# A four-layer transformer forward pass on one core: stage ends of the first layer type removed, work moved between stages and engines

## The chip, the cores and the metric

The kernel is one program for one core of a Trainium2 chip. Time is device time in microseconds (us), taken per execution. TensorE is called PE, VectorE DVE, ScalarE ACT, GpSimd POOL, and SP is the queue that loads weights from HBM. A PE row in the trace is one or more matmuls of one source line.

## The reference

A batch of one sequence with 512 tokens and model width 1024 passes through two layers of a first type and two of a second type. In the first type the input projection feeds three mixers, whose outputs are joined, projected and added to x, and an MLP follows:

```
def first_block(x, ...):
    for l in range(DEPTH):
        h = rms_norm(x, norm_mix[l])
        z = h @ w_in[l]
        (q_a, k_a, v_a, q_h, i_h, f_fw, f_bw, g_h, a_c, g_c) = jnp.split(z, splits, axis=-1)
        ...
        o_att = block_attention(q_a, k_a, v_a)              # 8 heads of 64, softmax over 512 keys
        o_hg = hgrn2_bidirectional(q_h, i_h, f_fw, f_bw, g_h, ...)   # 4 heads of 64, both directions
        o_cv = conformer_conv(a_c, g_c, conv_w[l], ...)     # 31 taps on 256 channels
        mix = jnp.concatenate([o_att, o_hg.astype(x.dtype), o_cv], axis=-1)
        x = x + mix @ w_out[l]
        h = rms_norm(x, norm_mlp[l])
        x = x + jnp.square(jax.nn.relu(h @ w_mlp_in[l])) @ w_mlp_out[l]
```

The recurrence, S_t = diag(f_t) S_{t-1} + k_t v_t and o_t = S_t^T q_t, runs forwards and backwards; the sum of both is normalised per head and multiplied by silu(g). The second type has four mixers (among them a gated linear recurrence with one direction and two attentions with masks), a gated sum of them, and an MLP. Everything is float32.

## The kernel before

**Tiles.** Activations lie transposed, features on the 128 partitions and the 512 tokens along the free dimension. A projection tile is 8 blocks of the contraction, three matmuls each: weights and activations are split into a high and a low part (`hH`, `hL`, `w_hi`, `w_lo`) and three of the four products are summed. ACT makes `w_hi` (L231), POOL `w_lo` (L261), one unit of 128 x 1024 at a time, three units ahead of PE. DVE takes each finished tile out of the two accumulators `acc` (`evacuate`), and PE may write an accumulator again when `acc_free` has counted that.

**Order.** Every engine has its own instruction stream, in the order in which the Python code issues it, and waits on semaphores. There is no scheduler: what stands behind a waiting instruction waits too.

**A layer of the first type** (`first_layer`) goes through these stages. `first_in`, 12 tiles: inputs of the convolution, forget gates, and q and v of the recurrence. DVE puts 30 of the 62 convolution taps behind these tiles (`CONV_EARLY`). Then two turns: PE transposes the recurrence's v tiles `Z[10]` and `Z[11]` into token order (`turn_pe`, L736) and ACT copies them back (`turn_act`, L744). Then the recurrence in two runs (`Recurrence`), run r on heads 2r and 2r+1. A run has 19 steps: for each direction nine levels with half width h = 256, 128, 64, ..., 1, and one last step for the diagonal. In a step with half width h, DVE subtracts a reference column from the summed log decays `cum` (the gap, L829), ACT takes its exponential (L880), DVE multiplies q and k by it (L838), PE makes the scores (L910), and two steps later DVE keeps them in `near` or `SS` (L857, L866). The levels with h = 256 and 128 are the far ones. Beside run 0 PE computes six tiles of `late_in` (the attention's q, k, v), which get their norm and rotation there (`rope_pe`, `norm_act`, `rope_dve`), beside run 1 the last two (the gate g). Each run ends with the products with the values (`pe_values`, L921).

**Turn to attention.** After run 1 every stream computes what is left of the heads' norms: PE sums squares (L1137, L1142), ACT makes the reciprocal roots (L1239, L1240), DVE multiplies and splits (L1360 to L1363, L435, L436). Then `finish` drains each engine and `after` makes each wait for the other two. Then PE turns the attention's v tile `Z[5]` and ACT copies it.

**Attention** (`PairAttention`) goes through 16 slots, four query blocks for each of four pairs of heads. In slot s, PE makes the scores of both heads (L585), DVE their negated maxima (L709), ACT the exponentials with their sums (L656). DVE in slot s+1 takes the reciprocal (L715) and scales both heads' rows (L720), PE in slot s+2 transposes them (L612), ACT copies (L675). After four slots PE makes the products with v (L629), and DVE takes the output of the pair (`take_output`, L1099, L1100). Beside slots 0 to 10 DVE puts the 32 remaining taps (L1288). The convolution's layer norm is spread over slots 11 to 15. No tile of a projection runs beside this attention. Then `out` and the MLP follow.

**The second type** uses the same classes: `Recurrence` with one direction beside `fox_in`, and `PairAttention` beside `stick_in` and `gate3`.

## Time and profile before

| | |
|---|---|
| time, median of 3 runs | 3814.58 us (3814.35 to 3814.77) |
| the profiled execution's own time | 3813.89 us |
| its span | 3812.6 us |
| mean granted PE clock | 0.977 of full speed |
| PE busy | 3653.6 us, 96% |
| DVE busy | 2175.0 us, 57% |
| ACT busy | 1305.1 us, 34% |
| chain that ended last | PE 83%, DVE 13%, issue 3%, ACT 2% |

Layer 0 of the first type fills about the first 750 us, and layer 1 repeats it about 700.6 us later. The clock is given as a share of 2.4 GHz, and 0.50 is 1.2 GHz. Rows of the timeline that follow each other overlap by some 0.08 us, so a DVE instruction of 0.69 us takes 0.60 of its stream.

### The profile page before, as it was taken

How to read it: one execution, taken by the hardware profiler on the slowest of the kernel's cores; microseconds unless marked ns; L12 is line 12 of the kernel's file. 1: busy time of each engine (PE TensorE's matmuls, PEld its weight loads, DVE VectorE, ACT ScalarE, POOL GpSimd, SP SyncE). 2: the span in 40 equal slices, each digit the busy share in tenths (PEclk: the TensorE clock that was granted, in tenths of full speed). 3: DMA queues.
4: the chain of work that ended last, by engine and by line, in shares of the span. 5: the costliest groups of instructions: out<-in, count | busy, mean ns of one | idle time of the engine just before them, and what ended most of it. 6: DMA issues, size and time to landing. Idle time of an engine off the chain costs nothing.

```text
span 3812.6 us, 44671 instructions
## 1 busy us (share of the span) xinstructions
PE 3653.6 (96%) x17862; PEld 2809.7 (74%) x17862; DVE 2175.0 (57%) x3018; ACT 1305.1 (34%) x2217; POOL 1292.0 (34%) x522
## 2 busy tenths in 40 slices
PE   8889999987899999999999999999999999999998
PEld 6646888865488888677777678887767777778887
DVE  7887565698764474633274485555553255365445
ACT  5345121343521122435333432123354433442212
POOL 3102444430044443132333244444213232334443
PEclk9889999997999999999999999999999999999999
DMA  4101333310033334122222133334112121223332
GB/s 137 40 12 45 97 97 96 94 61 23 13 96 97 96 98 136 34 63 60 78 62 76 52 88 100 94 100 145 57 34 78 58 81 61 67 72 94 99 94 83
DMA packets 81373, 292.38 MB, mean 77 GB/s; under 512 B 9712, under 2 KB 11152, under 8 KB 80656
## 3 DMA queue, kind: packets, MB, share of 16 engines
q1 hardware_dynamic: 78384, 278.49, 23.9%
q10 hardware_dynamic: 2784, 11.03, 0.9%
q8 instruction: 143, 2.34, 0.3%
q14 instruction: 62, 0.51, 0.0%
HBM read 285.30 MB, written 2.10 MB: 75 GB/s over the span
## 4 chain that ended last, share of the span: by engine, by line
PE 83%; DVE 13%; issue 3%; ACT 2%; DMA 0%; SPq 0%; DVEq 0%; ACTq 0%
PE acc L317 23%; PE acc L319 22%; PE acc L318 22%; PE banks L629 2%; PE banks L585 2%; PE banks L910 2%; DVE conv_c L1288 2%; PE banks L612 2%; PE banks L921 1%; DVE gap L829 1%; DVE QK L838 1%; DVE stat L709 1%; PE banks L1536 1%; DVE pair L387 1%; DVE probs L720 1%
## 5 line engine op out<-in xcount | busy, mean ns | idle before, releaser
L261 POOL TENSOR_TENSOR w_lo<-w_raw,w_hi 128x1024 fp32r<-128x1024 f32 x518 | 1291.8, 2495 | 2490.4 <-ACT w_hi L231 2490.4
L231 ACT ACTIVATE w_hi<-w_raw 128x1024 fp32r<-128x1024 f32 x518 | 548.7, 1060 | 1712.6 <-PE acc L319 1659.9
L317 PE MATMUL acc<-hH,w_hi 128*128 128x512 f32 x1776 | 731.9, 412 | 18.5 <-DVE sig L1921 6.6
L319 PE MATMUL acc<-hL,w_hi 128*128 128x512 f32 x1776 | 699.6, 394 | 0.0
L318 PE MATMUL acc<-hH,w_lo 128*128 128x512 f32 x1776 | 698.8, 393 | 0.0
L317 PEld LDWEIGHTS acc<-hH,w_hi 128*128 128x128 f32 x1776 | 337.5, 190 | 107.0 <-issue 32.9
L317 PE MATMUL acc<-H,w_hi 128*128 128x512 f32 x1024 | 400.4, 391 | 3.8 <-DVE L L379 3.8
L350 DVE TENSOR_TENSOR xT<-acc,xT 128x512 f32<-128x512 f32 x160 | 110.6, 691 | 514.3 <-PE acc L319 495.7
L317 PE MATMUL acc<-midH,w_hi 128*128 128x512 f32 x1024 | 400.3, 391 | 0.3
L318 PE MATMUL acc<-midH,w_lo 128*128 128x512 f32 x1024 | 398.7, 389 | 0.0
L319 PE MATMUL acc<-midL,w_hi 128*128 128x512 f32 x1024 | 398.5, 389 | 0.0
L319 PE MATMUL acc<-L,w_hi 128*128 128x512 f32 x1024 | 398.4, 389 | 0.0
L318 PE MATMUL acc<-H,w_lo 128*128 128x512 f32 x1024 | 398.4, 389 | 0.0
L319 PEld LDWEIGHTS acc<-hL,w_hi 128*128 128x128 f32 x1776 | 337.2, 190 | 73.8
L318 PEld LDWEIGHTS acc<-hH,w_lo 128*128 128x128 f32 x1776 | 338.3, 191 | 66.4 <-issue 4.3
L317 PEld LDWEIGHTS acc<-midH,w_hi 128*128 128x128 f32 x1024 | 192.2, 188 | 46.6 <-DVE midL L477 7.0
L317 PEld LDWEIGHTS acc<-H,w_hi 128*128 128x128 f32 x1024 | 192.2, 188 | 46.0 <-DVE L L379 5.5
L318 PEld LDWEIGHTS acc<-H,w_lo 128*128 128x128 f32 x1024 | 192.2, 188 | 40.6 <-issue 1.0
L319 PEld LDWEIGHTS acc<-midL,w_hi 128*128 128x128 f32 x1024 | 192.2, 188 | 40.2
L319 PEld LDWEIGHTS acc<-L,w_hi 128*128 128x128 f32 x1024 | 192.2, 188 | 40.0
L318 PEld LDWEIGHTS acc<-midH,w_lo 128*128 128x128 f32 x1024 | 192.3, 188 | 39.4
L476 DVE CAST midH<-relu_sb 128x512 fp32r<-128x512 f32 x64 | 160.2, 2504 | 2.2
(324 smaller groups left out, 4722.7 us busy)
## 6 DMA issues: line engine op xcount, KB each, us to landing
w_raw<-in_stream SPq DMA_DIRECT2D x518, 512.0 KB, 3.6
cw<-in_cmpw ACTq DMA_DIRECT2D x2, 2048.0 KB, 7.2
mixed<-in_cmpw ACTq DMA_DIRECT2D x2, 2048.0 KB, 12.7
x_tok<-in_x SPq DMA_DIRECT2D x2, 1024.0 KB, 7.3
out<-f_tok SPq DMA_DIRECT2D x8, 256.0 KB, 2.1
stack<-Z ACTq DMA_DIRECT2D x8, 128.0 KB, 2.3
stack<-Z ACTq DMA_DIRECT2D x8, 127.8 KB, 2.5
masks_f<-in_masks SPq DMA_DIRECT2D x1, 960.0 KB, 11.7
```

Of the source, the lines that this page charges most:

```text
L231: act.activation(w_hi[:, u % WB, 0:w], w_raw[:, u % 2, 0:w], ACT.Copy).then_inc(hi_split, 1)
L261: pool.tensor_tensor(w_lo[:, u % WB, 0:w], w_raw[:, u % 2, 0:w], w_hi[:, u % WB, 0:w], ALU.subtract)\
L317: pe.matmul(acc[n % 2][:, :], wh, H[:, k, :], start=(k == 0), stop=False)
L318: pe.matmul(acc[n % 2][:, :], wl, H[:, k, :], start=False, stop=False)
L319: last = pe.matmul(acc[n % 2][:, :], wh, Lo[:, k, :], start=False, stop=(k == nk - 1))
L350: dve.tensor_tensor(xT[:, i, :], a[:, :], xT[:, i, :], ALU.add).then_inc(up(free), 1)
L476: link(dve, dve.tensor_copy(midH[:, i, :], r))
L585: last = pe.matmul(self.score_banks[h % 3][:, 0:m], w["q"][r, qt * P:(qt + 1) * P], w["k"][r, lo * P:hi * P], start=True, stop=True, skip_ ...
L612: last = pe.transpose(self.turn_banks[n % 2][:, j * P:(j + 1) * P], self.P[:, s % 3, a, j * P:(j + 1) * P], ident)
L629: pe.matmul(self.out_bank[HD * a:HD * a + HD, cols], w["v"](kt, a), self.PT[:, a, kt, cols], start=(first and kt == 0), stop=True, skip_gr ...
L910: last = pe.matmul(scores, KK[r, jt * P:(jt + 1) * P], moving, start=(j == 0), stop=True, skip_group_check=True)
L1288: ins = dve.scalar_tensor_tensor(conv_c[:, j, :], src, vec[:, w:w + 1], conv_c[:, j, :], ALU.mult, ALU.add)
```

## The change

For a first-type layer both barriers are removed (`finish`, `after`). PE turns `Z[10]` and `Z[11]` in step 2 of run 0 and `Z[5]` in step 1 of run 1, into other banks; ACT copies them one step later. The first two heads' squares are summed in step 9 of run 1, and their roots taken in its step 11. What was left of the last two heads' norms, and the multiplications of all four, goes into slots 0, 1, 2 and 4 of the attention, and the 32 late taps are spread by `CONV_LATE` in place of 2 or 3 in each slot. ACT scales the second head's rows in the attention of the first type (`act_scale`), DVE the first head's.

For both types, a far level has no DVE gap: ACT takes the exponential straight from `cum` with the reference as its bias, in one instruction per block and half (2 for h = 256, 4 for h = 128), and one small DVE instruction per run makes the negated references. The output of a pair is taken out one slot later.

```diff
+CONV_LATE = [2, 2, 1, 3, 1, 4, 4, 4, 4, 4, 3]
...
-                    pe.wait_ge(self.p_normed, since(self.p_normed) + 2 * s + a + 1)
+                    if self.p_scaled is None:
+                        pe.wait_ge(self.p_normed, since(self.p_normed) + 2 * s + a + 1)
+                    elif a == 0:
+                        pe.wait_ge(self.p_normed, since(self.p_normed) + 2 * s + 2)
+                    else:
+                        pe.wait_ge(self.p_scaled, since(self.p_scaled) + s + 1)
...
+                    if self.p_scaled is not None and 1 <= slot <= self.n:
+                        self.act_scale(slot - 1)
...
+
+            def act_scale(self, s):
+                m, pr = self.span(s)[2], self.P[:, s % 3, 1, 0:self.span(s)[2]]
+                act.wait_ge(self.p_normed, since(self.p_normed) + 2 * s + 1)
+                act.activation(pr, pr, ACT.Copy, scale=self.stat[:, s % 3, 2, 1:2]).then_inc(up(self.p_scaled), 1)
...
-                    p = self.values_due(slot)
+                    p = self.values_due(slot - 1)
...
+                if self.p_scaled is not None:
+                    dve.reciprocal(rs, self.stat[:, s % 3, 1, :]).then_inc(up(self.p_normed), 1)
+                    dve.wait_ge(self.p_normed, since(self.p_normed) + 2 * s + 1)
+                    pr = self.P[:, s % 3, 0, 0:m]
+                    dve.tensor_scalar(pr, pr, rs[:, 0:1], None, ALU.mult).then_inc(up(self.p_normed), 1)
+                    return
...
+        FIRST_TURN_BANKS = (4, 5, 5)
...
+                dve.tensor_scalar(self.refs[:, run, 0:self.dirs, :], self.BB[run][:, :, P:T:P], -1.0, None, ALU.mult)\
+                    .then_inc(up(refs_ready), 1)
                 for s in range(self.n + 2):
-                    if s < self.n and self.steps[s][1]:
...
-                    i = (self.n - 1) * run + s
-                    act.wait_ge(gap_ready, since(gap_ready) + i + 1)
-                    h = self.steps[s][1]
+                    d, h = self.steps[s]
+                    if self.far(s):
+                        act.wait_ge(refs_ready, since(refs_ready) + run + 1)
+                        if s >= 2:
+                            act.wait_ge(terms_ready, since(terms_ready) + self.n * run + s - 1)
+                    else:
+                        act.wait_ge(gap_ready, since(gap_ready) + self.gaps(run, s) + 1)
                     for which in range(2):
-                        G = self.half(self.gap[:, s % 2, :], h, which)
-                        last = act.activation(G, G, ACT.Exp, scale=1.0 if which else -1.0)
+                        if self.far(s):
+                            for at in range(0, T, 2 * h):
+                                ref = (self.refs[:, run, d, (at + h) // P - 1:(at + h) // P] if which else
+                                       self.BB[run][:, d, at + h:at + h + 1])
+                                c = at + which * h
+                                last = act.activation(self.gap[:, s % 2, c:c + h],
+                                                      self.BB[run][:, d, 1 - d + c:1 - d + c + h], ACT.Exp,
+                                                      scale=1.0 if which else -1.0, bias=ref)
+                        else:
+                            G = self.half(self.gap[:, s % 2, :], h, which)
+                            last = act.activation(G, G, ACT.Exp, scale=1.0 if which else -1.0)
                     last.then_inc(up(decay_ready), 1)
...
-                    for n in (first_in.first + 10, first_in.first + 11):
-                        pe.wait_ge(acc_free[n % 2], n // 2 + 1)
-                    turn_pe([Z[:, 10, :], Z[:, 11, :]], 0)
...
+                        if s == 2:
+                            for n in (first_in.first + 10, first_in.first + 11):
+                                pe.wait_ge(acc_free[n % 2], n // 2 + 1)
+                            turn_pe([Z[:, 10, :], Z[:, 11, :]], 0, FIRST_TURN_BANKS)
...
-                    for r in range(2):
-                        rec.pe(r, Z[:, 8 + r, :], both_keys[:, r, :], late_in, None if r else rope_pe)
-                        if r:
+
+                    def second_run(s):
+                        if s == 1:
+                            n = late_in.first + 5
+                            pe.wait_ge(acc_free[n % 2], n // 2 + 1)
+                            pe.wait_ge(z_done, since(z_done) + 5)
+                            turn_pe([Z[:, 5, :]], 2, FIRST_TURN_BANKS)
+                        if s == 9:
                             pe.wait_ge(o_squared, since(o_squared) + 1)
                             pe.matmul(B[4][:, :], pair_ones, terms[:, 0, :], start=True, stop=True).then_inc(up(o_summed), 1)
-                            pe.wait_ge(z_done, since(z_done) + 5)
+                    for r in range(2):
+                        rec.pe(r, Z[:, 8 + r, :], both_keys[:, r, :], late_in, second_run if r else rope_pe)
+                        pe.wait_ge(v_ready, since(v_ready) + 2 + r)
                         rec.pe_values(r, [(a, lambda jt, a=a: v_tok[1 + r][:, jt, HD * a:HD * a + HD], B[4 + r],
                                            slice(HD * a, HD * a + HD)) for a in range(2)]).then_inc(up(o_ready), 1)
-                    pe.wait_ge(o_squared, since(o_squared) + 2)
-                    pe.matmul(B[5][:, :], pair_ones, terms[:, 1, :], start=True, stop=True).then_inc(up(o_summed), 1)
-                    finish(pe, "hgrn")
-                    after(pe, stages, "hgrn", act_finished, dve_finished)
-                    turn_pe([Z[:, 5, :]], 2)
-                    pe.wait_ge(v_ready, since(v_ready) + 3)
 
                     def conv_pe(slot):
+                        if slot == 1:
+                            pe.wait_ge(o_squared, since(o_squared) + 2)
+                            pe.matmul(B[5][:, :], pair_ones, terms[:, 1, :], start=True, stop=True).then_inc(up(o_summed), 1)
+                            pe.wait_ge(o_rstd, since(o_rstd) + 1)
+                        if slot == 4:
+                            pe.wait_ge(o_rstd, since(o_rstd) + 2)
...
-                    turn_act([v_tok[1], v_tok[2]], 0)
...
+                        if s == 3:
+                            turn_act([v_tok[1], v_tok[2]], 0, FIRST_TURN_BANKS)
...
+                        if s == 2:
+                            turn_act([v_tok[0]], 2, FIRST_TURN_BANKS)
...
+                        if s == 11:
+                            act.wait_ge(z_normed, since(z_normed) + 5)
+                            rstd_of_heads(0, tmp[:, :])
+
+                    def rstd_of_heads(r, rs):
+                        act.wait_ge(o_summed, since(o_summed) + r + 1)
+                        link(act, act.activation(rs, B[4 + r][:, :], ACT.Ln, bias=EPS, scale=1.0 / HD))
+                        act.activation(rs, rs, ACT.Exp, scale=-0.5).then_inc(up(o_rstd), 1)
...
                     for r in range(2):
+                        n = FIRST_TILE[layer, "late_in"] + 6 + r
+                        act.wait_ge(acc_free[n % 2], n // 2 + 1)
                         act.activation(pair[:, r, :], Z[:, 14 + r, :], ACT.Sigmoid).then_inc(up(gate_ready), 1)
...
-                    for r, rs in enumerate((tmp[:, :], terms[:, 2, :])):
-                        if r:
+
+                    def conv_act(slot):
+                        if slot == 0:
                             act.wait_ge(o_taken, since(o_taken) + 2)
                             act.activation(terms[:, 1, :], yt[:, 1, :], ACT.Square).then_inc(up(o_squared), 1)
-                        act.wait_ge(o_summed, since(o_summed) + r + 1)
-                        link(act, act.activation(rs, B[4 + r][:, :], ACT.Ln, bias=EPS, scale=1.0 / HD))
-                        act.activation(rs, rs, ACT.Exp, scale=-0.5).then_inc(up(o_rstd), 1)
-                    finish(act, "hgrn")
-                    after(act, stages, "hgrn", pe_finished, dve_finished)
-                    turn_act([v_tok[0]], 2)
-
-                    def conv_act(slot):
+                        if slot == 1:
+                            rstd_of_heads(1, terms[:, 2, :])
...
-                    for r in range(2):
-                        dve.wait_ge(gate_ready, since(gate_ready) + r + 1)
-                        dve.tensor_tensor(Z[:, 14 + r, :], pair[:, r, :], Z[:, 14 + r, :], ALU.mult)
-                    dve.wait_ge(o_ready, since(o_ready) + 2)
-                    dve.tensor_copy(yt[:, 1, :], B[5][:, :]).then_inc(up(o_taken), 1)
-                    for r, rs in enumerate((tmp[:, :], terms[:, 2, :])):
...
-                    finish(dve, "hgrn")
-                    after(dve, stages, "hgrn", pe_finished, act_finished)
...
                     def conv_dve(slot):
-                        left = len(taps) - early
+                        if slot == 0:
+                            dve.wait_ge(o_ready, since(o_ready) + 2)
+                            dve.tensor_copy(yt[:, 1, :], B[5][:, :]).then_inc(up(o_taken), 1)
+                        if slot == 1:
+                            for r in range(2):
+                                dve.wait_ge(gate_ready, since(gate_ready) + r + 1)
+                                dve.tensor_tensor(Z[:, 14 + r, :], pair[:, r, :], Z[:, 14 + r, :], ALU.mult)
+                        if slot == 2:
+                            heads_normed(0, tmp[:, :])
+                        if slot == 4:
+                            heads_normed(1, terms[:, 2, :])
                         if slot < CONV_NORM:
-                            conv_taps(early + slot * left // CONV_NORM, early + (slot + 1) * left // CONV_NORM)
+                            conv_taps(early + sum(CONV_LATE[:slot]), early + sum(CONV_LATE[:slot + 1]))
```

Three places in the streams. The first is DVE between run 1 and the attention in layer 0, before (`near` and `banks` belong to the recurrence, `stat` and `probs` to the attention, `yt` holds the heads):

```order
L866 COPY_PREDICATED near<-masks,banks 128x1024
L1354 TENSOR_TENSOR Z<-pair,Z 128x512 x2
L1356 COPY yt<-banks 128x512
L1360 SCALAR_TENSOR_TENSOR yt<-yt,vec_1,tmp 128x512
L1362 TENSOR_TENSOR yt<-yt,Z 128x512
L435 CAST hH<-yt 128x512
L436 TENSOR_TENSOR hL<-yt,hH 128x512
L1360 SCALAR_TENSOR_TENSOR yt<-yt,vec_1,terms 128x512
L1362 TENSOR_TENSOR yt<-yt,Z 128x512
```

and of the changed kernel:

```order
L888 COPY_PREDICATED near<-masks,banks 128x1024
L711 TENSOR_REDUCE stat<-banks 128x1 x2
L1416 COPY yt<-banks 128x512
L1341 SCALAR_TENSOR_TENSOR conv_c<-conv_u,vec_1,conv_c 128x512 x2
L711 TENSOR_REDUCE stat<-banks 128x1 x2
L718 RECIPROCAL stat<-stat 128x2
L721 TENSOR_SCALAR probs<-probs,stat 128x512
L1420 TENSOR_TENSOR Z<-pair,Z 128x512 x2
L1341 SCALAR_TENSOR_TENSOR conv_c<-conv_u,vec_1,conv_c 128x512 x2
L711 TENSOR_REDUCE stat<-banks 128x1 x2
L718 RECIPROCAL stat<-stat 128x2
L721 TENSOR_SCALAR probs<-probs,stat 128x512
```

The attention's first maxima now follow the last kept scores at once, and the copy, the gates' products and the norms stand between maxima. The second place is PE at the start of run 0, before:

```order
L318 MATMUL acc<-hH,w_lo 128x512
L319 MATMUL acc<-hL,w_hi 128x512
L736 MATMUL banks<-C,Z 128x128 x8
L317 MATMUL acc<-hH,w_hi 128x512
L318 MATMUL acc<-hH,w_lo 128x512
L319 MATMUL acc<-hL,w_hi 128x512
L317 MATMUL acc<-hH,w_hi 128x512
```

and of the changed kernel, where the nine matmuls of `late_in`'s step 0 (its last three stand first here) follow `first_in` directly and the run's first scores come behind them:

```order
L318 MATMUL acc<-hH,w_hi 128x512
L319 MATMUL acc<-hH,w_lo 128x512
L320 MATMUL acc<-hL,w_hi 128x512
L945 MATMUL banks<-QK 128x256 x4
L318 MATMUL acc<-hH,w_hi 128x512
L319 MATMUL acc<-hH,w_lo 128x512
L320 MATMUL acc<-hL,w_hi 128x512
L318 MATMUL acc<-hH,w_hi 128x512
```

and further on, at step 2 of the run:

```order
L318 MATMUL acc<-hH,w_hi 128x512
L319 MATMUL acc<-hH,w_lo 128x512
L320 MATMUL acc<-hL,w_hi 128x512
L745 MATMUL banks<-C,Z 128x128 x8
L945 MATMUL banks<-QK 128x64 x8
L318 MATMUL acc<-hH,w_hi 128x512
```

The eight transposes moved from between `first_in` and `late_in` to just ahead of the third step's scores. The third place is ACT between run 1 and the attention, before:

```order
L1233 ACT_TABLE_LOAD
L1239 ACTIVATE tmp<-banks 128x512
L1240 ACTIVATE tmp<-tmp 128x512
L1237 ACTIVATE terms<-yt 128x512
L1239 ACTIVATE terms<-banks 128x512
L1240 ACTIVATE terms<-terms 128x512
L744 ACTIVATE Z<-banks 128x512
L656 ACTIVATE probs,stat<-banks,stat 128x512 x6
L675 ACTIVATE probsT<-banks 128x4x128 x2
```

and of the changed kernel:

```order
L1292 ACT_TABLE_LOAD
L653 ACTIVATE probs,stat<-banks,stat 128x512 x2
L1297 ACTIVATE terms<-yt 128x512
L653 ACTIVATE probs,stat<-banks,stat 128x512 x2
L660 ACTIVATE probs<-probs,stat 128x512
L1283 ACTIVATE terms<-banks 128x512
L1284 ACTIVATE terms<-terms 128x512
L653 ACTIVATE probs,stat<-banks,stat 128x512 x2
L660 ACTIVATE probs<-probs,stat 128x512
L677 ACTIVATE probsT<-banks 128x4x128 x2
```

The first heads' root (`tmp`) is gone from here, the second's (`terms`) stands behind the exponentials of slots 0 and 1, and each slot has one scaling of `probs` more.

## Rows read from the trace of the kernel before

**Rows 1.** The page, part 1: busy time of each engine, share of the span, instructions.
```profile
PE 3653.6 (96%) x17862; PEld 2809.7 (74%) x17862; DVE 2175.0 (57%) x3018; ACT 1305.1 (34%) x2217; POOL 1292.0 (34%) x522
```

**Rows 2.** Busy us by stage; then PE clock, DMA share, GB/s. Last row: layer 1.
```profile
131.70:162.80 31.10, 31.04 (x196) 22.15 (x196) 30.89 (x38) 14.16 (x27) 7.63 (x3) 1.00 0.17 51
...
190.40:232.50 42.10, 36.68 (x322) 26.38 (x323) 39.99 (x56) 17.44 (x37) 5.84 (x2) 0.92 0.09 26
232.50:247.20 14.70, 8.21 (x76) 5.74 (x76) 6.24 (x10) 3.68 (x6) 0.00 (x0) 0.73 0.00 1
247.20:295.70 48.50, 44.03 (x156) 19.04 (x156) 46.79 (x89) 25.01 (x62) 0.00 (x0) 0.83 0.00 0
295.70:326.60 30.90, 25.45 (x108) 11.06 (x106) 17.96 (x39) 20.52 (x42) 0.00 (x0) 0.89 0.00 1
...
947.80:996.30 48.50, 43.40 (x157) 18.80 (x157) 46.82 (x89) 25.06 (x63) 0.00 (x0) 0.88 0.00 1
```

**Rows 3.** Timeline, PE and one of ACT: start, us, form, count [idle before <- releaser].
```profile
101.80 1.94 PE L736 MATMUL banks<-C,Z 128*128 128x128 f32 x8 [9.22 <-DVE Z L1272]
...
102.92 0.60 ACT L744 ACTIVATE Z<-banks 128x512 f32<-128x512 f32 x1 [8.61 <-PE banks L736]
...
104.42 0.79 PE L317 MATMUL acc<-hH,w_hi 128*128 128x512 f32 x1 [0.69 <-ACT Z L744]
...
108.56 1.80 PE L910 MATMUL banks<-QK 64*128 64x256 f32 x8
110.29 0.50 PE L317 MATMUL acc<-hH,w_hi 128*128 128x512 f32 x1
```

**Rows 4.** Timeline of DVE, and of POOL for one row, run 0.
```profile
105.55 1.28 DVE L829 TENSOR_TENSOR gap<-cum 128x512 f32<-128x512 f32 x2
107.02 0.69 DVE L838 TENSOR_TENSOR QK<-Z,gap 128x512 f32<-128x512 f32 x1 [0.18 <-ACT gap L880]
...
144.50 2.36 POOL L261 TENSOR_TENSOR w_lo<-w_raw,w_hi 128x1024 fp32r<-128x1024 f32 x1 [9.20 <-ACT w_hi L231]
...
144.97 2.43 DVE L829 TENSOR_TENSOR gap<-cum 128x512 f32<-128x512 f32 x1
```

**Rows 5.** Chain of waits, both runs' value products: start, us, what.
```profile
183.40 6.16 PE banks L921 x64
...
232.50 3.84 PE banks L921 x64
```

**Rows 6.** PE timeline between run 1 and attention.
```profile
230.43 2.07 PE L1137 MATMUL banks<-terms,C 128*128 128x512 f32 x2
...
243.16 1.09 PE L736 MATMUL banks<-C,Z 128*128 128x128 f32 x4 [4.26 <-DVEq L492]
```

**Rows 7.** DVE timeline, same stretch.
```profile
230.55 1.29 DVE L866 COPY_PREDICATED near<-masks,banks 128x1024 f32<-128x1024 uint8 x1 [0.53 <-PE banks L910]
...
236.97 0.74 DVE L1360 SCALAR_TENSOR_TENSOR yt<-yt,vec,tmp 128x512 f32<-128x512 f32 x1
...
238.94 0.69 DVE L436 TENSOR_TENSOR hL<-yt,hH 128x512 fp32r<-128x512 f32 x1
...
247.22 1.29 DVE L709 TENSOR_REDUCE stat<-banks 128x1 f32<-128x512 f32 x2 [4.26 <-PE banks L585]
```

**Rows 8.** DVE timeline, in an attention slot, and the end of slot 10.
```profile
260.04 0.88 DVE L720 TENSOR_SCALAR probs<-probs,stat 128x512 f32<-128x512 f32 x2
...
294.36 0.68 DVE L1099 CAST hH<-banks 128x512 fp32r<-128x512 f32 x1
```

**Rows 9.** PE timeline, attention, matmuls at the low clock.
```profile
245.02 8.36 PE L585 MATMUL banks<-Z 64*128 64x512 f32 x12 [0.77 <-ACT Z L744]
253.30 1.97 PE L612 MATMUL banks<-C,probs 128*128 128x128 f32 x8
...
320.13 6.04 PE L629 MATMUL banks<-probsT,Z 128*64 128x512 f32 x16 [0.69 <-ACT probsT L675]
```

**Rows 10.** Waits of PE, second type's recurrence begins: us, times, longest.
```profile
PE banks L910 <- DVE QK L838: 2.5, 1, 2.5
```

More of the change, by code:

```diff
@@ L760, in __init__, with far, gaps @@
                 self.n = len(self.steps)
+            def far(self, s):
+                return self.steps[s][1] >= P
+            def gaps(self, run, s):
+                one = [h > 0 and h < P for _, h in self.steps]
+                return run * sum(one) + sum(one[:s])
             @staticmethod
@@ L1491, in second_layer @@
                                     extra=Z0[:, 8:12, :].rearrange("p (i a) t -> p i a t", a=2), take_output=split_pair)
-                rec = Recurrence(1, [BB[:, r:r + 1] for r in range(2)], gap, QK, near, SS, [(5 * NK, 10)] * 2)
+                rec = Recurrence(1, [BB[:, r:r + 1] for r in range(2)], gap, QK, near, SS, refs, [(5 * NK, 10)] * 2)
                 stick_banks = [(B[0], B[1], B[4]), (B[2], B[3], B[5])]
```

44 lines of the change are left out of this document (20 added, 24 removed).

## The prediction

> **What bounds the kernel now.** I read the page first. PE is busy for 3653.6 us, 96% [rows 1], so the change can only act where PE is not what ends last. The busy time by stage [rows 2] finds these places. From 131.7 to 162.8 PE (31.04 of 31.10) and DVE (30.89) are both full. In run 1 of the recurrence (190.4 to 232.5) DVE is the fuller, 39.99 of 42.1 against 36.68, at a clock of 0.92. Between run 1 and the attention (232.5 to 247.2) nobody is: PE 8.21 and DVE 6.24 of 14.7. In slots 0 to 10 of the attention DVE has 46.79 of 48.5, and the last row shows the same in layer 1. In slots 11 to 15 (295.7 to 326.6) a slot is a round of dependent steps, with PE at 25.45, ACT at 20.52 and DVE at 17.96 of 30.9. The timelines and the chain then give what starts and ends each stretch, and the prices.
>
> **a. Start of run 0.** Before, PE idles 9.22 us until the Z of tile 11, turns for 1.94 (101.80), and has `late_in`'s nine matmuls from 104.42, at the low level (0.63 each against 0.39 to 0.50 later); the first scores stand at 108.56 [rows 3]. In the changed kernel the nine matmuls need no turn. They fit into the time in which PE idled, so they no longer delay anything, and the first scores wait for DVE alone. DVE had two gaps until some 106.8 and then the first QK product [rows 4]. The two gaps (1.2 of its stream) go, a reference of about 0.1 comes, and ACT's first exponentials start when the taps end. That puts the first product at 106.4 and the scores at about 107.5, when ACT's four exponentials took 1.33 for two steps: 1.1 us earlier. Against it stand two terms. The turns, 1.94 at the low level and a little over half of that at the high one, now lie in a stretch in which PE is full: +1.1. And the clock: before, PE worked from 101.80 on and was at the high level at 110.29 [rows 3]. Now it has some 4 us of matmuls before about 102 and an idle of 5 us until 107.5, so I take it that the clock is low at 107.5 and rises as late after steady work began as before, near 116. Against the high level from 110.3 that is 4 to 6 us of matmuls at half speed, so +2.0 to +3.0; I take +2.0. The sum is -1.1 + 1.1 + 2.0, about +1.9. The ends are 0 (the nine matmuls hold the clock's rise where it was) and +3.5.
>
> **b. Far gaps.** Per run four gaps of 0.60 go to ACT, which gets more instructions but has 17.44 of 42.1 busy [rows 2]. They save only where DVE is what is late. In run 0 PE is full too until 162.8, so nothing. In run 1 the first direction's two come at its start with DVE behind, the other two in its middle: 2 x 0.60 with a third of the others lost, less 0.2 for the references, gives about -0.9, between -1.2 and 0. One of run 0's gaps lasted 2.43 us instead of 0.64, beside a POOL instruction of 2.36 that began 0.47 earlier (144.50) [rows 4]. I book that at nothing more than 0.60, as the product behind it would then meet the same POOL instruction.
> The Trainium skill's page "SBUF — State Buffer", section "SBUF: two separate sides", says that DVE and GpSimd share a port pair which is taken as an exclusive lock for a whole instruction, by a DVE operation with two SBUF inputs among others. The gap and the QK product both have two SBUF inputs, and by this rule the stall passes to the product. If the stall left with the gap, that one would save 2.4 and not 0.6, and the sum would be 1.8 per first-type layer better.
>
> **c. The turn to attention.** DVE's last kept scores begin at 230.55 and end at 231.84 [rows 7]. The value products of run 1 begin at 232.50, behind an o_sum pair of 2.07 (230.43) [rows 5, 6] that now stands in step 9. So they start at 231.9 in place of 232.5. They took 3.84 us at the high level and 6.16 in run 0, at the low one [rows 5]; PE has gaps before them, so I take 5.0. Scores of slot 0 follow at once (12 matmuls took 8.36 at the low level [rows 9], so the pair of slot 0 with what DVE needs first is about 1.4). First maximum: 231.9 + 5.0 + 1.3 = 238.2, against 247.22 [rows 7]. That is -9.0, between -10.2 (all high) and -6.9. What leaves is the barrier (4.26 of idle before the turn of `Z[5]` at 243.16 [rows 6]), its turn and copy, and the wait of DVE for the norms; what is late next is the value products and slot 0's scores.
>
> **d. Slots 0 to 10.** What left the turn comes here. DVE's heads chain runs from 236.97 to 239.55 for one head, 2.6 us [rows 7]: 5.2 for two, 0.6 for the copy and 1.2 for the gates, 7.0 in all. A slot of DVE is two maxima 1.2, reciprocal 0.19, two scalings 0.80 and two or three taps, about 2.0 [rows 7, 8]. The scaling moved to ACT takes 0.40 off each of ten slots, -4.0, and slot 10 no longer contains a take-out (the second pair's, two instructions of 0.6 from 294.36 on [rows 8]: 1.3). So DVE has 46.8 - 4.0 - 1.3 + 7.0 = 48.5 of work. With 0.8 idle (it had 1.7, part of it in slots where it now has less slack to lose) the stretch is 49.3 against 48.5: +0.8, between 0 and +2.5. The upper end has PE in slot 1 waiting for the square of the second heads, which passes DVE's copy behind the maxima and ACT's exponentials. The scaling on ACT is covered: ACT had 25.01 in eleven slots [rows 2], 2.3 a slot, and with one more instruction on 128x512 of 0.60 (102.92 [rows 3]) 2.9, against 4.4 on DVE.
>
> **e. Slots 11 to 15.** Here the round counts, not the load. The take-out of a pair comes one slot later, and the 1.3 us now stand ahead of the last slot's scaling: +1.3. Each slot's DVE part is 0.40 shorter, but ACT's scaling of 0.60 takes its place in the round beside the first head's transposes: -0.5 in all. The drain at the end goes: -0.3. Sum +0.5, between -1.5 and +1.5.
>
> **Sum.** Per first-type layer +1.9 - 0.9 - 9.0 + 0.8 + 0.5 = -6.7, so -13.4 for two. The second type has no part of c and d; its runs lose the same gaps beside projections, where PE is full. Only at the start of its recurrence does PE wait for DVE's first product, 2.5 us in the one look shown [rows 10], with two gaps ahead of it: -1.0 a layer (0 to -2.0), so -2.0. The later take-out costs nothing there, as PE has projection tiles to do. Together -15.4: the profiled execution goes from 3813.9 to 3798.5. The median stood 0.7 above it, and I keep the same figure rounded for the median, 3799.
>
> **Rivals.**
> *R1, bigger.* The clock is high again at 110 and through the value products (a 0, c -10.3), both far gaps of run 1 count in full (b -1.2), d stays at +0.8 and the tail's round shortens by ACT and DVE scaling side by side (e -1.0). Sum -11.7 a layer, with -2 for the second type -25.4: 3788.5. For it: layer 1 had a clock of 0.88 where layer 0 had 0.83 in slots 0 to 10 [rows 2]. Against it: PE idles 9.22 us before run 0, and nothing of that idle becomes work for PE beyond nine matmuls.
> *R2, about the same.* DVE is full in slots 0 to 10 both before and after, so the work moved there is paid in full and ACT's scaling only changes which engine is late, as PE must now wait for a product of each. Then d is 7.0 - 1.3 = +5.7, e +1.5, a +1.9, b -0.5, c -9.0: -0.4 a layer, and with -3 for the second type -3.8 in all: 3810. For it: 46.79 of 48.5. Against it: the scaling's output is needed only two slots later in PE's order, and ACT is idle half of the time.
> *R3, slower.* The attention has no projection beside it, and before it fell to the low level only for its first slots: scores 8.36 for twelve, 1.97 for eight transposes [rows 9]. At that level a slot costs PE 2.79 + 1.97 + a fourth of the value products' 6.04 (320.13 [rows 9]), 6.3 us, against DVE's 48.5 / 11 = 4.4. Each slot that stays low beyond those of before costs 1.9. Before, PE idled and began the attention at 243.16; if the new waits (for the square in slot 1, for two engines' scalings) keep it from steady work, the level stays low. The 6.7 of a layer are used up at 3.5 extra slots; with 8 extra it is +8.5 a layer, 3829. Against it: it returned to the high level by itself in layer 0 although slots 0 to 3 had gaps.
> *R4, no turn is saved:* a semaphore of the moved work ties the first slot to the norms. The streams speak against it: the maxima follow the last kept scores, and only PE's slots 1 and 4 wait for heads. I give it no chance of its own beside R2.
>
> **How the numbers follow.** Forecast 0.55, R1 0.20, R2 0.18, R3 0.07. What a measurement can tell from no change here is 0.2%, 7.6 us. The forecast's own range is 3793 to 3805. R1 lies around 3788, of which the part below 3785 is left out; R2 stands at 3810 and is taken in up to 3811. The range is 3785 to 3811. Faster needs less than 3807: forecast and R1, and a third of R2, 0.81; same 0.14, slower 0.05.
>
> **What would show it.** First maxima of layer 0 some 9 us earlier than 247.22, behind value products that start near 231.9. Slot 0 to slot 10 about 49.3 us with DVE over 48 busy and PE high for most of it. First scores of run 0 near 107.5, and the clock's rise after 112. If the time falls by over 20 us, the clock terms (a, c) were wrong; if by less than 8, d or e was: PE rows of transposes would then be released by ACT's scaling or by DVE with idle before them in every slot.

## The result and the profile after

The changed kernel takes 3849.77 us (median of 4 runs, 3848.39 to 3850.61), the kernel before 3814.68: a ratio of 1.0091 with a 95% interval of 1.0076 to 1.0106, so 35 us slower (times of the kernel before vary a little from one comparison to the next, so each ratio below is to the runs of its own comparison). The forecast was 3799 with a range of 3785 to 3811. Both the sign and the range were wrong, and none of the four rivals names what happened. The profiled execution has a span of 3849.1 against 3812.6, +36.5.

Where the 36.5 lie is seen from the page's first row and from the groups by line, which answer to [rows 1]. First the page of the changed kernel, PE's busy time:

```profile
PE 3695.8 (96%) x17862; PEld 2819.0 (73%) x17862; DVE 2149.1 (56%) x2970; ACT 1331.6 (35%) x2273; POOL 1291.9 (34%) x522
```

PE has the same 17862 instructions and is busy 42 us longer. The groups of PE by line (count, busy us, mean ns), of the kernel before:

```profile
L317 PE MATMUL acc<-hH,w_hi 128*128 128x512 f32 x1776 | 731.9, 412 | 18.5 <-DVE sig L1921 6.6 <-DVE Z L1272 4.3 <-DVE yt L1943 3.3
...
L317 PE MATMUL acc<-H,w_hi 128*128 128x512 f32 x1024 | 400.4, 391 | 3.8 <-DVE L L379 3.8
L317 PE MATMUL acc<-midH,w_hi 128*128 128x512 f32 x1024 | 400.3, 391 | 0.3
L318 PE MATMUL acc<-midH,w_lo 128*128 128x512 f32 x1024 | 398.7, 389 | 0.0
```

and of the changed kernel:

```profile
L318 PE MATMUL acc<-hH,w_hi 128*128 128x512 f32 x1776 | 732.1, 412 | 22.9 <-DVE Z L1325 10.5 <-DVE sig L1976 6.6 <-DVE yt L1998 2.8
...
L318 PE MATMUL acc<-H,w_hi 128*128 128x512 f32 x1024 | 406.2, 397 | 3.3 <-DVE L L380 3.3
L318 PE MATMUL acc<-midH,w_hi 128*128 128x512 f32 x1024 | 405.9, 396 | 0.0
...
L319 PE MATMUL acc<-midH,w_lo 128*128 128x512 f32 x1024 | 404.1, 395 | 0.0
```

The loss is in the MLPs, which the change does not touch. The matmuls that read `hH` are as fast as before (412 ns), those that read `H`, `L`, `midH` and `midL` take 5 to 6 ns more, at a granted clock of 1.00 in both. Six groups of 1024 give 34.1 us; the three groups of the second type's joins (`yH`, `yL`, 256 each) go from 300.4 to 304.3, 3.9 more. That is 38.0, more than the whole difference.

What the prediction did speak of came out smaller than forecast, but with the right sign. These are starts in layer 0, read from the timelines:

| | before | after | difference | forecast |
|---|---|---|---|---|
| first scores of run 0 | 108.56 | 107.38 | -1.2 | -1.1 |
| first maximum of the attention | 247.22 | 238.46 | -8.8 | -8.0 (a, b, c) |
| slots 0 to 10 | 48.46 | 52.31 | +3.9 | +0.8 (d) |
| slots 11 to 15, to the first matmul of `out` | 30.90 | 32.32 | +1.4 | +0.5 (e) |
| layer to there | | | -3.5 | -6.7 |

PE's timeline at the start of run 0, which answers to [rows 3]:

```profile
98.88 0.63 PE L320 MATMUL acc<-hL,w_hi 128*128 128x512 f32 x1
107.38 2.08 PE L945 MATMUL banks<-QK 64*128 64x256 f32 x8 [7.87 <-DVE QK L860]
109.39 0.80 PE L318 MATMUL acc<-hH,w_hi 128*128 128x512 f32 x1
...
112.54 0.63 PE L319 MATMUL acc<-hH,w_lo 128*128 128x512 f32 x1
...
113.36 0.71 PE L945 MATMUL banks<-QK 64*128 64x128 f32 x8
...
116.91 1.03 PE L745 MATMUL banks<-C,Z 128*128 128x128 f32 x8
```

`late_in`'s nine matmuls lie in what was idle time, the last at 98.88. The first scores come after 7.87 of idle, and PE is at 1.2 GHz (0.63 a matmul) until about 113, where before it was at 2.4 GHz from 110. The DVE timeline of the attention, which answers to [rows 7]:

```profile
238.46 1.29 DVE L711 TENSOR_REDUCE stat<-banks 128x1 f32<-128x512 f32 x2 [7.14 <-PE banks L575]
...
270.99 1.29 DVE L711 TENSOR_REDUCE stat<-banks 128x1 f32<-128x512 f32 x2 [2.04 <-PE banks L575]
...
275.44 0.68 DVE L1134 CAST hH<-banks 128x512 fp32r<-128x512 f32 x1
...
290.77 1.29 DVE L711 TENSOR_REDUCE stat<-banks 128x1 f32<-128x512 f32 x2 [1.27 <-PE banks L575]
```

and busy times of both parts of it (us, then PE, PEld, DVE, ACT, POOL, then PE's clock), which answer to the rows 247.20 and 295.70 of [rows 2]:

```profile
238.46:290.77 52.31, 44.66 (x151) 19.02 (x150) 48.34 (x87) 32.66 (x75) 0.00 (x0) 0.84 0.00 0
290.77:323.09 32.32, 26.64 (x113) 12.66 (x113) 16.46 (x33) 23.90 (x48) 0.00 (x0) 0.84 0.00 1
```

DVE's work in slots 0 to 10 is 48.34, against 48.5 in the forecast. What is new are its waits for scores, 2.04 ahead of slot 7 and 1.27 ahead of slot 11, 3.3 us. The chain shows what stands in them, here around slot 7:

```profile
260.07 0.61 DVE stat L711
...
260.73 0.56 issue
261.29 0.86 ACT probs L653 x3
262.15 0.61 ACT probs L660
262.76 0.98 ACT probsT L677 x2
...
263.79 5.08 PE banks L624 x16
268.88 1.02 PE banks L607 x8
269.90 1.11 PE banks L575 x4
271.01 1.27 DVE stat L711 x2
```

Value products (L624) wait for the copies (L677), these for ACT's scaling of another slot (L660), and the next scores stand behind the value products. The kernel before has the same round without the 0.61 of L660, and its take-out, 1.3 of DVE's work, lies in the time in which DVE would wait; now it stands at 275.44, behind the wait. In the kernel before, the wait ahead of slot 7 is therefore short:

```profile
277.65 1.29 DVE L709 TENSOR_REDUCE stat<-banks 128x1 f32<-128x512 f32 x2 [0.62 <-PE banks L585]
```

### The profile page after: what moved, and what is told of

Its sections match the earlier page's. It is cut to its first block, busy times and chain, and to the rows that moved or that the text cites. A ratio compares the mean times of both kernels' runs of the same rounds, so it can differ in the third digit from the quotient of the medians.

```text
span 3849.1 us, 44685 instructions
## 1 busy us (share of the span) xinstructions
PE 3695.8 (96%) x17862; PEld 2819.0 (73%) x17862; DVE 2149.1 (56%) x2970; ACT 1331.6 (35%) x2273; POOL 1291.9 (34%) x522
## 4 chain that ended last, share of the span: by engine, by line
PE 84%; DVE 12%; issue 2%; ACT 2%; DMA 0%; SPq 0%; ACTq 0%; DVEq 0%
PE acc L318 23%; PE acc L320 22%; PE acc L319 22%; PE banks L945 2%; PE banks L624 2%; PE banks L575 2%; DVE conv_c L1341 2%; PE banks L607 2%; PE banks L956 1%; DVE stat L711 1%; PE banks L1591 1%; DVE pair L388 1%; DVE QK L860 1%; PE banks L582 0%; PE banks L1688 0%
```

## The experiments

**Theory.** `refs`, 48 bytes for each partition and a filling to 128, is allocated before the buffers of the layers. It moves all of them by 128 bytes: `midH` from byte 122752 to 122880, `yH` from 130688 to 130816, while `hH` (18560), `w_hi` (61568) and `w_lo` (73856) stay. Modulo 256 all of these were at 128 before; now `midH`, `midL`, `H`, `L`, `yH` and `yL` are at 0. The rival is that the moved work leaves something that slows the MLPs down.

**The bytes.** The changed kernel:

```diff
         refs = sb("refs", [P, 2, 2, NT - 1])
+        sb("skew", [P, 128], U8)
```

> The changed kernel with 128 unused bytes behind `refs`, so that every buffer allocated after it lies 256 bytes further than before the change, not 128. Theory A (place): the matmuls of the MLPs and of the second type's joins read `H`, `L`, `midH`, `midL`, `yH`, `yL`, which the 128 bytes of `refs` moved; each takes 5.6 ns longer, 6912 of them, 38 us. With 256 bytes they are back: MLP matmuls at 389 ns in place of 395, and the time falls from 3849.8 to some 3812 (3809 to 3815). Rival B (the moved work or the ACT scaling leaves PE or its supply in another state for the MLPs): the bytes do nothing, 3849.8.

Measured: 11 runs, median 3817.27 (3809.45 to 3821.99), ratio to before 1.0005 (0.9996 to 1.0014). The profiled execution has a span of 3808.4, 40.7 less than with `refs` alone, and the MLPs are back:

```profile
L318 PE MATMUL acc<-H,w_hi 128*128 128x512 f32 x1024 | 400.4, 391 | 3.8 <-DVE L L380 3.8
L318 PE MATMUL acc<-midH,w_hi 128*128 128x512 f32 x1024 | 400.3, 391 | 0.2
```

Theory A holds. The runs lie in two groups, four at 3809.5 to 3810.6 and seven at 3817.2 to 3822.0, and the profile is of the first. So the median says that the change with its layout put right is no faster than the kernel before; only the lower group is, by 2.7 to 3.8 us. What sets the groups apart was not settled, so what follows goes by stages of the traces, each of them one execution.

The kernel before, with 128 bytes at the same place:

```diff
         lb_gap = sb("lb_gap", [P, 2, 4])
+        sb("skew", [P, 128], U8)
```

> The kernel before with 128 unused bytes at the place where the change puts `refs`, and nothing else. Theory A: 3814.7 + 38 = 3853 (3848 to 3856), MLP matmuls at 395 ns and those that read `hH` and `hL` as before. Rival B: 3814.7, no change.

Measured: 3851.77, ratio 1.0100 (1.0085 to 1.0114), MLP matmuls at 395 to 397 ns:

```profile
L317 PE MATMUL acc<-H,w_hi 128*128 128x512 f32 x1024 | 406.1, 397 | 3.3 <-DVE L L379 3.3
```

128 unused bytes alone do to the kernel before what the whole change did.

The bytes ahead of everything (`xT` is the first buffer):

```diff
+        sb("skew", [P, 128], U8)
         xT = sb("xT", [P, NK, T])
```

> The kernel before with 128 unused bytes ahead of the first buffer, so that all buffers, those of the weights too, move by 128 bytes. Theory A1 (the address of the moving operand itself counts): the 5520 matmuls that read `hH` and `hL` slow down as well, 12432 x 5.6 ns = 70 us, 3884. Theory A2 (the distance between the moving operand's address and the weights' counts): nothing changes, 3814.7.

Measured: 3813.22, ratio 0.9998 (0.9989 to 1.0007). Theory A2: an address by itself is neither good nor bad.

The weights alone:

```diff
+        sb("skew", [P, 128], U8)
         w_raw = sb("w_raw", [P, 2, UNIT])
...
+        sb("skew2", [P, 128], U8)
         C = sb("C", [P, len(CONSTS), P])
```

> The kernel before with 128 unused bytes ahead of `w_raw`, `w_hi` and `w_lo`, and 128 more behind them, so that the weights alone move by 128 bytes and all behind them by 256. Theory A1 (the address of the moving operand itself counts): nothing changes, 3814.7. Theory A2 (the distance to the weights counts): all 12432 matmuls slow down, 3884.

Measured: 3875.52, ratio 1.0161 (1.0145 to 1.0177), 62 us and not the 70 of theory A2. Now the matmuls that read `hH` are slower too; PE by line:

```profile
L319 PE MATMUL acc<-hH,w_hi 128*128 128x512 f32 x1776 | 741.0, 417 | 15.9 <-DVE sig L1923 6.2 <-DVE Z L1274 3.2 <-DVE yt L1945 2.6
L321 PE MATMUL acc<-hL,w_hi 128*128 128x512 f32 x1776 | 709.2, 399 | 0.0
...
L319 PE MATMUL acc<-H,w_hi 128*128 128x512 f32 x1024 | 406.2, 397 | 3.3 <-DVE L L381 3.3
```

399 against 394 ns for `hL`. What counts is the distance between the address of the moving operand and that of the weights, modulo 256. `w_raw`, `w_hi` and `w_lo` always moved together, so it was not tested apart which of them matters. But accesses of other engines do not explain it: in the MLPs, the starts of successive matmuls that read `midH` or `midL`, taken only where they are less than 300 ns apart, no instruction of DVE, ACT or POOL runs between them and no DMA packet began in the 1.5 us before, lie 226.7 ns apart in the trace of the kernel before and 233.1 in that of the changed one (357 and 297 pairs). Two more distances, with 64 and 32 bytes in the kernel before, without a filling:

```diff
         lb_gap = sb("lb_gap", [P, 2, 4])
+        ctx.enter_context(nc.sbuf_tensor("skew", [P, 64], U8))
```

> The kernel before with 64 unused bytes at the place where the change puts `refs`. The moving operands of MLPs and joins then lie 64 bytes off the weights' residue modulo 256, not 128. Theory A (any distance other than 0 modulo 256 costs the same): 3814 + 37 = 3851. Theory B (64 bytes is the unit, and the cost grows with the distance): between 3825 and 3840. Theory C (only 128 is bad): 3814.

> The kernel before with 32 unused bytes at the place where the change puts `refs`. Theory A (any distance other than 0 modulo 256): 3851. Theory B (a unit of 64 bytes, so that 32 leaves a part of each row off it): more than with 64 bytes or about the same, 3825 to 3860. Theory C (only 128 is bad): 3814.

Measured: 3829.39 (3 runs), ratio 1.0041 (1.0027 to 1.0056), with 64 bytes; 3858.75 (2 runs, 3855.14 and 3862.36), ratio 1.0118 (1.0100 to 1.0137), with 32. In the traces the group `midH,w_lo` takes 389 ns at distance 0, 391 at 64, 395 at 128 and 395 at 32; at 64 the groups that read the low part (`midL`, `L`) take 394. First 64, then 32:

```profile
L319 PE MATMUL acc<-midL,w_hi 128*128 128x512 f32 x1024 | 403.3, 394 | 0.0
```
```profile
L319 PE MATMUL acc<-midL,w_hi 128*128 128x512 f32 x1024 | 404.4, 395 | 0.0
```

The six groups of the MLPs together take 13.8 us more than before at 64, 35.9 at 32 and 34.1 at 128. So 64 costs less than half of 128, and 32, the smallest, as much as 128. The two runs at 32 are a little slower still, which these groups do not show. Neither theory A nor C holds; B fits, in that 32 costs more than 64, but the cost does not grow with the distance, and other distances were not tried.

**ACT's scaling.** All further kernels have the 256 bytes; stages are of layer 0, and of the changed kernel with 256 bytes they are: run 0's scores to the last value products 123.75, slots 0 to 10 52.29, slots 11 to 15 32.30.

```diff
-                att = PairAttention(..., take_output=split_pair, p_scaled=p_scaled)
+                att = PairAttention(..., take_output=split_pair)
```

> The changed kernel with the buffers at 256 bytes, and both heads' rows scaled by DVE again. There slots 0 to 10 take 52.3 us and slots 11 to 15 take 32.3. Theory A (ACT's scaling stands ahead of its copies, so that PE waits for `probsT`, and gives back what it saves on DVE): those waits vanish, slots 0 to 10 take DVE's work, 46.8 - 1.3 + 7.0 = 52.5, and 0.5 to 1.0 idle, 53.0 to 53.5, slots 11 to 15 some 31.5; the time changes by less than 2 us. Theory B (the scaling on ACT saves its 0.40 a slot as forecast, something else costs): slots 0 to 10 take 4 us more, 56.3, and the time is 8 us longer.

Measured: 3820.40, ratio 1.0019 (1.0010 to 1.0028). Slots 0 to 10 take 56.48, slots 11 to 15 31.83, and the first matmul of `out` in layer 1 comes 7.6 us later than with the scaling on ACT. Theory B: DVE's work in slots 0 to 10 grows by 4.0, to 52.3, its idle time stays at about 4 (4.2 against 3.9), and so the scaling on ACT does save its 0.40 a slot.

```diff
-                    if self.p_scaled is not None and 1 <= slot <= self.n:
-                        self.act_scale(slot - 1)
                     if slot >= 2:
                         for a in range(2):
                             self.act_turn(slot - 2, a)
+                    if self.p_scaled is not None and 1 <= slot <= self.n:
+                        self.act_scale(slot - 1)
```

> The changed kernel with the buffers at 256 bytes, and ACT's scaling put behind its two copies of `probsT` in a slot instead of ahead of them. Theory A (PE's waits for `probsT`, 0.6 us in about every second slot, come from the order on ACT): they vanish, slots 0 to 10 take 50 to 51 us in place of 52.3, slots 11 to 15 up to 1 less, and the time is 3 to 6 us shorter. Theory B (what holds PE is its low clock in slots 3 to 5 and 7): the waits move to another place and slots 0 to 10 stay at 52 or more.

Measured: 3809.92, ratio 0.9990 (0.9981 to 0.9999). Nine of the ten runs lie at 3807.8 to 3810.7, where the lower group of the kernel without this edit lies too; the profiled one is the tenth and slowest, 3814.62, so its stages may not be those of the others. In it slots 0 to 10 take 51.48, 0.8 less and not 1.3 to 2.3; slots 11 to 15 32.46, no gain. PE's waits in the attention, with the scaling ahead and then behind:

```profile
PE banks L607 <- ACT probsT L677: 6.6, 6, 2.3
PE banks L575 <- ACT probs L653: 3.9, 4, 1.8
PE banks L624 <- ACT probsT L677: 2.5, 3, 1.1
```
```profile
PE banks L575 <- ACT probs L653: 3.8, 4, 1.7
PE banks L607 <- ACT probsT L677: 2.2, 1, 2.2
PE banks L607 <- ACT probs L660: 2.1, 4, 0.5
PE banks L624 <- ACT probsT L677: 1.2, 2, 0.7
```

The waits for copies fall from 9.1 to 3.4, but 2.1 come back as waits for the scaling itself (L660). The order on ACT costs something, and in this execution most of the 3.3 us is not from it; its clock in slots 0 to 10 is 0.80 where it was 0.84, which may hide a part of the gain.

**The take-out.**

```diff
-                    p = self.values_due(slot - 1)
+                    p = self.values_due(slot)
```

> The changed kernel with the buffers at 256 bytes, and the output of a pair taken out in its old slot, in both layer types. Theory A (the later take-out keeps the output bank from PE in the second type, some 0.4 us at each pair's value products): the second type's two layers get back 2 to 3 us; in the first type slots 0 to 10 hold 1.3 more and slots 11 to 15 as much less. In all 2 to 3 us shorter. Theory B (the take-out is hidden in both): no change within 1 us.

Measured: 3805.67, ratio 0.9979 (0.9970 to 0.9988). In layer 0 slots 0 to 10 take 52.95 and slots 11 to 15 31.64, together 84.59, exactly as with the later take-out (84.59): the 1.3 us moved 0.7 from one part to the other, and the rest fell into DVE's wait. From the first matmul of `out` in layer 1 to the end this execution takes 2786.4, against 2789.4 with the later take-out and 2786.3 in the kernel before. That is theory A's 3 us, but the last kernel below has the old slot as well and takes 2789.4. And where only the first type was edited, the same part took 2789.4 (turns), 2792.4 (scaling on DVE), 2793.9 (scaling behind the copies) and 2794.2 (added matmul): the same code varies by 4.8 from trace to trace. So the place of the gain is not shown. That the old slot gains something is shown: all ten runs (3803.1 to 3808.7) are faster than the fastest of the eleven without it (3809.45).

**The turns.** PE's eight transposes and ACT's two copies ahead of `late_in` again, PE without a wait for the copies:

```diff
...
                     first_in.products()
+                    for n in (first_in.first + 10, first_in.first + 11):
+                        pe.wait_ge(acc_free[n % 2], n // 2 + 1)
+                    turn_pe([Z[:, 10, :], Z[:, 11, :]], 0, FIRST_TURN_BANKS)
                     late_in = Group(layer, "late_in")
...
```

> The changed kernel with the buffers at 256 bytes, and the turns of `Z[10]` and `Z[11]` ahead of `late_in` again. There the first scores stand at 107.4 and run 0 and 1 take 123.8 from them to the last value products. Theory A (the nine matmuls that run while PE would idle leave PE at 1.2 GHz when run 0 begins, and the turns lie in a full stretch): scores at 108.5 at the latest, 1.1 later, but the two runs take 121.0 to 121.8, so that the values start 1 to 2 us earlier; 2 to 4 us in all. Theory B (the clock rises at the same distance from the first scores either way): the values start as late or up to 1.1 later.

Measured: 3811.72 (3802.68 to 3812.83), ratio 0.9991 (0.9982 to 1.0001). PE at the start of run 0:

```profile
102.07 1.94 PE L745 MATMUL banks<-C,Z 128*128 128x128 f32 x8 [9.23 <-DVE Z L1324]
...
106.80 0.51 PE L319 MATMUL acc<-hH,w_lo 128*128 128x512 f32 x1
107.15 0.40 PE L320 MATMUL acc<-hL,w_hi 128*128 128x512 f32 x1
107.70 1.13 PE L945 MATMUL banks<-QK 64*128 64x256 f32 x8 [0.16 <-DVE QK L860]
```

The scores are only 0.3 later, the clock is back at 2.4 GHz from 107, and the two runs take 120.80 in place of 123.75: theory A, 2.6 us earlier at the value products. But slots 0 to 10 then take 55.19. The value products ahead of slot 11 fall into a low stretch, and DVE waits longer for the scores behind them:

```profile
282.27 6.46 PE L624 MATMUL banks<-probsT,Z 128*64 128x512 f32 x16 [0.18 <-ACT probsT L677]
```
```profile
290.84 1.29 DVE L711 TENSOR_REDUCE stat<-banks 128x1 f32<-128x512 f32 x2 [4.07 <-PE banks L575]
```

6.46 in place of 3.65, 4.07 in place of 1.27: the same 2.8. The first maximum came 2.4 us earlier (235.65 against 238.07), and slots 0 to 10 then take 2.9 more, in both layers. This is one execution; three of the ten runs lie at 3802.7 to 3807.0, and whether they give it back too is not known.

**The clock in the attention.**

```diff
...
+                        if 2 <= slot < CONV_NORM:
+                            pe.matmul(acc[0][:, :], pair_ones, C[:, 0:4, :], start=True, stop=True)
```

> The changed kernel with the buffers at 256 bytes, and in slots 2 to 10 of the first type's attention one more matmul of PE, 128x512 into an accumulator that nothing reads (0.5 us at the high clock). Theory A (PE's idle time in the slots lets its clock fall, 0.84 over slots 0 to 10, and the waits of DVE in slots 7 and 11, 3.3 us, come from the products at 1.2 GHz): the clock goes to 0.92 or more, slots 0 to 10 take 49 to 51 us in place of 52.3. Theory B (the waits come from PE's queue, whatever its clock): PE has 9 x 0.5 us more in front of what DVE waits for, and slots 0 to 10 take 53 to 56.

Measured: 3819.91, ratio 1.0015 (1.0006 to 1.0024). The added matmul stands in the trace as two rows and takes 1.02, not 0.5. The clock of slots 0 to 10 does rise, from 0.84 to 0.91, and they take 53.95, as theory B said: DVE's waits ahead of slots 7 and 11 grow by 0.8 and 0.9, about one added matmul each. But the value products in front of them take 5.00 and 3.65, as without the edit (5.06 and 3.65), so the higher clock did not reach the place that theory A was about, and A is not refuted. The run with the turns, where they took 6.46, shows that a low stretch there is paid in full.

**All three together.** Take-out in its old slot, turns ahead, scaling behind the copies: the three edits above in one kernel.

> The changed kernel with the buffers at 256 bytes, the take-out in its old slot, the turns ahead of `late_in`, and ACT's scaling behind its copies. Theory A (the three are independent): against the same kernel without them 3 us from the take-out in the second type, 3 us a layer from the turns before run 1 ends, 0.9 a layer from the scaling; 3798 to 3802, faster than the kernel before by 12 to 16. Theory B (what the turns win before the attention is given back in its slot 10, as in the run with the turns alone, 2.8 us): 3803 to 3806.

Measured: 5 runs, 3794.86 (3788.90 to 3799.69), ratio 0.9949 (0.9937 to 0.9962), faster than both kernels. The two parts of the attention in layer 0:

```profile
234.75:285.38 50.63, 44.89 (x156) 18.70 (x155) 49.57 (x90) 32.65 (x75) 0.00 (x0) 0.87 0.00 0
285.38:315.85 30.47, 25.47 (x109) 11.06 (x107) 15.26 (x32) 23.71 (x48) 0.00 (x0) 0.89 0.00 1
```

81.1 for the attention against 84.6, and `out` begins at 315.85, 10.7 us before the kernel before; layer 1 gains as much again. DVE is busy for 49.57 of 50.63. Two things differ from the run with the turns alone: the take-out fills what was DVE's wait, and the value products of slot 10 are at the high level,

```profile
279.02 3.65 PE L624 MATMUL banks<-probsT,Z 128*64 128x512 f32 x16 [0.52 <-ACT probsT L677]
```

where they had taken 6.46. The second is worth 2.8 of the 4.6 us between the two; whether the edits brought it about or where the low stretch happened to fall, no run tells. With one edit alone, the first matmul of `out` in layer 1 stands at 1020.7 (take-out), 1019.8 (turns) and 1019.3 (scaling), against 1019.0 with none of them; with all three it stands at 1005.4. The three are not independent, and together they are worth more than apart, which neither theory said.

## Why the prediction was wrong

**The step that failed** is a term put at nothing: `refs` was priced as "a reference of about 0.1" of DVE, and the layout that its allocation moves was given no term. It measured +38.0 us in the trace, and by itself, in the kernel before, 38.6 (3851.77 against 3813.21). It stood in the diff, as a new buffer allocated ahead of the layers' own. That the MLPs, whose code is the same, would also take the same time was assumed without a word, and no rival doubts it.

With the buffers at 256 bytes the forecast would still have been too good: -4.2 in the trace, which is of the lower group, where -15.4 was forecast; the median, 3817.27, stays outside the range. By its own terms:

**a**, +1.9 forecast (its three terms add up to 2.0). The first scores at 107.38 (forecast 107.5) and the low level until about 113 (forecast near 116) are as described. Near the end of run 0's scores the same row stands at 167.94 with 256 bytes and at 166.80 before, so +1.1. The place of the turns and the clock, put at 3.1 together, cost 2.6 against the run with the turns ahead, whose first scores are 0.3 later. The mechanism was right, the size a little large.

**b**, -0.9 forecast. Not measured apart. Run 1's first scores stand 0.3 later than before (190.68 against 190.39) and its last 0.9 earlier (223.08 against 223.94): 1.2 gained in run 1, so it was hardly less. Another 0.8 was gained over run 0's value products, between its last scores and run 1's first, which no term had.

**c**, -9.0 forecast. The value products begin at 231.46 (forecast, without a and b, 231.9), take 5.8 (5.0), and the first maximum comes 1.2 behind them (1.3), at 238.46. From the start of the value products to the first maximum it is 7.0 in place of 14.8, -7.8, where 6.3 in place of 14.7 was forecast: right in kind, 0.6 short.

**d**, +0.8 forecast, +3.9 measured. DVE's work was right to 0.2 us. The idle time was not: it was set to 0.8 because DVE had 1.7 before, and it is 4.0. The prediction took a loaded engine's idle time for slack. It comes from a round (copies, value products, transposes, scores) that stands twice in slots 0 to 10. ACT's scaling does not make it: with both heads on DVE it is 4.2. With the take-out in its old slot it is 3.1, so taking 1.3 of work away there saved 0.7 and not 1.3. What makes the rest of the difference to the kernel before was not taken apart.

**e**, +0.5 forecast, +1.4 measured, between its ends (+1.5). The two edits undone one by one give its parts: the later take-out costs 0.7 (forecast 1.3), and the scaling on ACT costs 0.5 where -0.5 was forecast.

**The second type**, -1.0 a layer forecast. From the first matmul of `out` in layer 1 to the end it took 2789.4 with 256 bytes against 2786.3, +3.1 for two layers in these two executions. The four other traces with the same code there have 2789.4 to 2794.2, and the kernel before with all buffers moved has 2786.0, so it is slower each time, but by how much is not settled. At the start of its recurrence PE waits 2.1 and not 2.5 [rows 10]. One reason can be read in the changed kernel's trace (with 256 bytes it is the same, 2.28): the instruction for the references, 128x3, stands where a gap stood and is stretched like it, beside a POOL instruction of 2.39 that began 0.13 earlier:

```profile
3137.42 2.39 POOL L262 TENSOR_TENSOR w_lo<-w_raw,w_hi 128x1024 fp32r<-128x1024 f32 x1 [4.12 <-ACT w_hi L232]
```
```profile
3137.55 2.29 DVE L838 TENSOR_SCALAR refs<-cum 128x3 f32<-128x3 f32 x1
```

In the first type the same instruction, 128x6, takes 0.16, with no POOL instruction beside it. So a stall does pass to what stands in the gap's place, as was assumed in b. The Trainium skill's page "SBUF — State Buffer", section "SBUF: two separate sides", says that VectorE and GpSimd share a port pair that one instruction holds for its whole length. The trace agrees: the 3 columns are done at 3139.84, when POOL's instruction is (3139.81). The page names DVE instructions with two SBUF inputs or in a two-port mode; this one has a single SBUF input, and no trace shows its mode. Whether and where the 3.1 us are lost is open beyond that.

**The rivals.** The time came out slower, but not by R3: the clock over slots 0 to 10 is 0.84, as before (0.83), with low stretches in other slots. R2 came near for e (+1.5) and was right that d would be dear, but for the wrong reason: ACT's scaling kept its saving in slots 0 to 10 (56.48 without it).

## What to carry to other kernels

A new buffer, however small, is part of a change's price: list the addresses of matmul operands before and after, and keep the moving operand and the weights at the same residue modulo 256, the only one of four distances that cost nothing here. When work is moved on an engine that is nearly full, look at where it waits and not how long: work that lies in a wait can be free, and taking it away need not shorten the stretch (1.3 us less work saved 0.7 there, and cost 0.7 in the next part). Parts that gain little singly can win together (3794.86 against 3805.67 at best), so a change of five parts is worth taking apart before it is given up.

## What the runs showed of the hardware

A float32r matmul of 128x512 took 389 ns in the trace (391 for the first of three) where moving operand and weights had the same address modulo 256, 391 to 394 at a distance of 64, and 395 (396 to 397 for the first) at 128 and at 32, at a clock of 1.00. Following each other in the MLPs, their starts lie 0.227 us apart at 0, 0.229 at 64 and 0.233 at 128 and 32. Moving both by 128 bytes changed nothing. A DVE instruction on 3 columns took 2.29 us beside a POOL instruction of 2.39; one on 6 columns took 0.16 without one.
